# A decoder trunk on one core: the first shift and scale computed from a turned matrix, with 24 units between

## What is computed

```python
for l in range(DEPTH):
    ada = (silu(c) @ w_ada[l] + b_ada[l])           # 2048 -> 6 * 2048
    sh_m, sc_m, g_m, sh_f, sc_f, g_f = split(ada, 6)
    h = x * (1 + sc_m) + sh_m
    y = hybrid_mixer(h, ...)          # h @ w_in[l] (6672 columns), three head groups, @ w_out[l]
    x = layer_norm(ALPHA * x + (1 + g_m) * y, ...)
    h = x * (1 + sc_f) + sh_f
    y = square(relu(h @ w1[l])) @ w2[l]             # 2048 -> 8192 -> 2048
    x = layer_norm(ALPHA * x + (1 + g_f) * y, ...)
```

## Time and profile before

| engine | busy us | share | instructions |
|---|---|---|---|
| TensorE (PE) | 2392.7 | 96% | 13077 |
| TensorE weight load | 2071.0 | 83% | 13077 |
| VectorE (DVE) | 1934.9 | 78% | 2130 |
| ScalarE (ACT) | 1158.8 | 46% | 1504 |
| GpSimd (POOL) | 167.4 | 7% | 120 |

### The profile page before, as it was taken

One profiled execution on the slowest core, in us unless ns is written; L12 is line 12 of the kernel. 1 busy time (PEld: TensorE's weight loads), 2 busy tenths in 40 slices (PEclk: granted clock), 3 DMA queues, 4 the chain that ended last, 5 costly groups with the idle time before them and its releaser, 6 DMA issues.

```text
span 2496.2 us, 32892 instructions
## 1 busy us (share of the span) xinstructions
PE 2392.7 (96%) x13077; PEld 2071.0 (83%) x13077; DVE 1934.9 (78%) x2130; ACT 1158.8 (46%) x1504; POOL 167.4 (7%) x120
## 2 busy tenths in 40 slices
PE   2599999999999999999999999999999999999998
PEld 2599988888888888888879998888888888888886
DVE  7889898877898898889886578778888565655657
ACT  0264475545434435434436446655543443443442
POOL 0002100010011011010010110001001101101001
PEclk9999999999999999999999999999999999999999
DMA  9998577877898898999866546678788666656663
GB/s 388 393 336 300 148 267 261 292 273 270 291 345 308 290 348 306 316 315 313 296 201 177 155 118 202 225 261 282 253 289 301 188 190 193 186 189 192 186 192 119
DMA packets 205054, 633.78 MB, mean 254 GB/s; under 512 B 20237, under 2 KB 20965, under 8 KB 203621
## 3 DMA queue, kind: packets, MB, share of 16 engines
q1 hardware_dynamic: 200320, 614.80, 73.1%
q0 software_dynamic: 3008, 16.32, 1.7%
q10 hardware_dynamic: 1572, 0.56, 0.1%
HBM read 629.50 MB, written 2.10 MB: 253 GB/s over the span
## 4 chain that ended last, share of the span: by engine, by line
PE 90%; DVE 5%; DMA 2%; issue 1%; ACT 1%; SPq 0%; DVEq 0%; ACTq 0%
PE PS L1658 46%; PE PS L1684 17%; PE PS L1686 8%; PE PS L1626 8%; PE PS L1667 4%; DMA RAW<-in_w_ada 2%; PE PS L1640 2%; DVE ACC L1082 1%; DVE WL L1091 1%; PE PS L1715 1%; PE PS L1558 1%; PE PS L1591 1%; DVE CV L1298 0%; DVE ACC L985 0%; DVE MS L1315 0%
## 5 line engine op out<-in xcount | busy, mean ns | idle before, releaser
L686 ACT ACTIVATE WH<-RAW 128x1024 fp32r<-128x1024 f32 (+1 forms) x800 | 831.8, 1044 | 1082.6 <-PE PS L1658 554.6
L1091 DVE TENSOR_TENSOR WL<-RAW,WH 128x1024 fp32r<-128x1024 f32 (+1 forms) x800 | 992.0, 1247 | 431.8 <-ACT WH L686 430.6
L1684 PE MATMUL PS<-HT,WH 128*128 128x512 f32 x1792 | 632.5, 398 | 0.0
L1686 PE MATMUL PS<-HT,WL 128*128 128x256 f32 x1792 | 502.5, 280 | 0.0
L1684 PEld LDWEIGHTS PS<-HT,WH 128*128 128x128 f32 x1792 | 336.5, 188 | 82.3 <-issue 0.5
L985 DVE SCALAR_TENSOR_TENSOR ACC<-ADR,CT,ACC 128x1024 f32<-128x1024 f32 x300 | 392.0, 1307 | 12.3 <-DMA ADR<-in_w_ada 10.4
L1658 PE MATMUL PS<-WH,T2h 128*128 128x512 f32 x1208 | 374.2, 391 | 0.0
L1658 PE MATMUL PS<-WL,T2h 128*128 128x512 f32 x1208 | 372.1, 389 | 0.0
L1658 PE MATMUL PS<-WH,T2l 128*128 128x512 f32 x1208 | 372.0, 389 | 0.0
L1686 PEld LDWEIGHTS PS<-HT,WL 128*128 128x128 f32 x1792 | 338.4, 189 | 0.7 <-issue 0.5
L1658 PE MATMUL PS<-WH,HT 128*128 128x512 f32 x1024 | 288.7, 395 | 0.6 <-issue 0.6
(11 more groups left out here) (297 smaller groups left out, 2035.1 us busy)
## 6 DMA issues: line engine op xcount, KB each, us to landing
RAW<-in_w SPq DMA_DIRECT2D x512, 512.0 KB, 4.1
ADR<-in_w_ada SPq DMA_DIRECT2D x320, 512.0 KB, 5.5
RAW<-in_w_in SPq DMA_DIRECT2D x192, 512.0 KB, 3.9
RAW<-in_w_ada SPq DMA_DIRECT2D x64, 512.0 KB, 15.9
RAW<-in_w_out SPq DMA_DIRECT2D x64, 512.0 KB, 4.9
RAW<-in_w_in SPq DMA_DIRECT2D x32, 264.0 KB, 2.7
GB<-in_b_ada POOLq DMA_DIRECT2D x8, 512.0 KB, 7.3
LNG<-in_ln_g POOLq DMA_DIRECT2D x4, 1024.0 KB, 6.9
```

Source lines behind the costliest of these rows:

```text
L686: act.activation(WH[:, wh_slot(layer, n), 0:w], RAW[:, k, 0:w], ACT.Copy).then_inc(hi_done.sem, 1)
L1091: tt(WL[:, k, 0:w], RAW[:, k, 0:w], WH[:, wh_slot(layer, n), 0:w].bitcast(F32), ALU.subtract).then_inc(lo_done.sem, 1)
L1684: mm(bank(p, j)[:, :], WH[:, wh, cols], HT[:, kt, :, :], start=kt == 0, stop=False, skip_group_check=True)
L1686: ins = mm(bank(p, j)[:, SEQ:2 * SEQ], WL[:, wl, cols], HTh[:, kt, :], start=False, stop=kt == KT - 1, skip_group_check=True)
```

## The change

Quarters 0 to 3 are no longer blocks of 1024 columns. The host lays the first 4096 columns of layer 0's w_ada out as 32 tiles of 128 by 2048 (`ada_first`): a tile has 128 outputs on the partitions and all 2048 inputs along the row. 28 of the tiles go to VectorE: one instruction multiplies the tile by CROW (silu of c, the same on all partitions) and writes the row sums, which are 128 outputs, straight into a column of ADA (`dot`). Four tiles, the first of groups 1 to 4, go to TensorE, as 16 small products each (`first_dot`). x also comes turned from the host (`x_turned`), so that h tiles are made from XT and not from transposes.

The tiles are ordered in eight groups of four, which give shift and scale for two kt each. After a group, its columns are set (`first_cols`), two h tiles are made (`first_tiles`), and units are done: two of pass 0 in groups 0 to 3, two of pass 0 and two of pass 1 in groups 4 to 7. So 24 units are in the queues before the loops begin, which skip them (EARLY). The tiles have four slots (FT) of 1 MB; a slot is loaded again when its tile has been used.

What stood in the first half of pass 1 of layer 0 moves to the second half (PRE), the scaling of X to unit 31, and TensorE waits for LFl ahead of pass 2. Quarter 6 moves from units 0 to 18 to 24 to 35, quarter 7 to 36 to 50, 8 is spread thinly over 51 to 91, 4 moves to 107 to 125, 5 to 126 to 140. X and part of the constants are loaded later, by GpSimd. The counts of the semaphores are adapted; this part is left out here.

```diff
-PRO_SLOTS = 16
+PRO_SLOTS = 4
+FIRST = [[(1, 1), (0, 0), (0, 1), (1, 0)] if 1 <= b <= 4 else [(0, 0), (0, 1), (1, 0), (1, 1)] for b in range(8)]
+FIRST_TILES = [(b, 2 * b + j, which) for b in range(8) for j, which in FIRST[b]]
+BY_TENSOR = [4 * b for b in range(1, 5)]
+BY_VECTOR = [i for i in range(32) if i not in BY_TENSOR]
+FIRST_UNITS = [[(0, 2 * b), (0, 2 * b + 1)] + ([(1, 2 * b - 8), (1, 2 * b - 7)] if b >= 4 else []) for b in range(8)]
+FIRST_ORDER = [u for units in FIRST_UNITS for u in units]
+EARLY = len(FIRST_ORDER)
+PASS0_END = FIRST_ORDER.index((0, 15)) + 1
+PRE = {1: 8, 3: 9, 4: 10, 8: 12, 9: 13, 11: 14, 15: 15}
...
-ADA_PLAN = [[(6, 0, 18), (7, 19, 34), (8, 35, 50), (9, 75, 92), (4, 93, 106), (5, 107, 134),
+ADA_PLAN = [[(6, 24, 35), (7, 36, 50), (8, 51, 92), (9, 93, 106), (4, 107, 125), (5, 126, 140),
...
+SPARSE = [51, 54, 57, 60, 63, 67, 71, 75, 78, 80, 82, 84, 85, 87, 89, 91]
...
+        XT = sb("XT", [P, KT, 2, SEQ], at=place["at"])
...
+        FT = sb("FT", [P, PRO_SLOTS, D], at=t2h_at)
+        CROW = W("CROW", 24, [P, D])
...
+        def tile_used(i):
+
+            if i in BY_TENSOR:
+                return pro_pe.sem, BY_TENSOR.index(i) + 1
+            return pro_dot.sem, BY_VECTOR.index(i) + 1
...
-                if layer == 0 and n < RAW_SLOTS:
-                    sp.wait_ge(ada_mac.sem, 2 + 64 - PRO_SLOTS + n + 1)
-                else:
+                if layer or n >= RAW_SLOTS:
...
-            for a in range(64):
-                if a >= PRO_SLOTS:
-                    sp.wait_ge(ada_mac.sem, a - PRO_SLOTS + 3)
-                dst, arrived = pro_slot(a)
-                sp.dma_start(dst, w_ada_r[(a % 16) * P:(a % 16 + 1) * P, (a // 16) * UW:(a // 16 + 1) * UW]
-                             ).then_inc(arrived, 16)
+            sp.dma_start(CROW[:, :], c.squeeze(0).partition_broadcast(P)).then_inc(pro_crow.sem, 16)
+            n = 0
+            for b in range(8):
+                for i in range(4 * b, 4 * b + 4):
+                    if i >= PRO_SLOTS:
+                        sp.wait_ge(*tile_used(i - PRO_SLOTS))
+                    sp.dma_start(FT[:, i % PRO_SLOTS, :], ada_first[i]).then_inc(pro_tile[i % PRO_SLOTS].sem, 16)
+                    if i % 8 == 0:
+                        t0 = i // 2
+                        sp.dma_start(XT[:, t0:t0 + 4, 1, :], x_turned[t0 * P:(t0 + 4) * P, :].rearrange(
+                            "(t p) n -> p t n", p=P)).then_inc(pro_xt.sem, 16)
+                for p, kt in FIRST_UNITS[b]:
+                    raw_load(0, n, w_in_r[kt * P:(kt + 1) * P, COL0[p]:COL0[p] + UW])
+                    n += 1
...
+            pool.wait_ge(pro_dot.sem, 14)
+            for dst, src in ((LMs[:, :], consts[:, K_LM:K_LM + 1024]), (MLR[:, :], consts[:, K_ML:K_LM]),
+                             (K[:, K_DG:], consts[:, K_DG:K_KEEP])):
+                pool.dma_start(dst, src).then_inc(pro_k.sem, 16)
+            pool.wait_ge(pro_dot.sem, len(BY_VECTOR))
...
+            act.wait_ge(pro_crow.sem, 16)
+            act.activation(CROW[:, :], CROW[:, :], ACT.Silu).then_inc(pro_silu.sem, 1)
...
+            def first_tiles(b):
+
+                act.wait_ge(pro_cols.sem, b + 1)
+                act.wait_ge(pro_xt.sem, 16 * (b // 2 + 1))
+                for kt in (2 * b, 2 * b + 1):
+                    cols, bias, scale = XT[:, kt, 1, :], SH[:, 0, kt:kt + 1], SC[:, 0, kt:kt + 1]
+                    act.activation(HTh[:, kt, :], cols, ACT.Identity, bias=bias, scale=scale).then_inc(hT_hi.sem, 1)
+                    if kt >= 4:
+                        act.wait_ge(hT_ready.sem, hT_ready.at(0, kt - 3))
+                    act.activation(TX[:, kt % 4, :], cols, ACT.Identity, bias=bias, scale=scale
+                                   ).then_inc(hT_tx.sem, 1)
...
+            act.wait_ge(pro_pt.sem, 1)
             act.activation(ACT_IDLE[:, :], PT[:, 0:1], ACT.Identity)
-            for n in range(2):
-                hi_split(0, n)
-            h_tiles(0, 0, 0)
-            for n in range(2, W_SLOTS):
+            n = 0
+            for b in range(8):
+                first_tiles(b)
+                for _ in FIRST_UNITS[b]:
+                    hi_split(0, n)
+                    n += 1
+                if b == 1:
+                    act.wait_ge(pro_dve.sem, 1)
+                    act.activation(LX[:, :], LX[:, :], ACT.Exp).then_inc(pro_act.sem, 1)
+                    act.wait_ge(pro_dve.sem, 2)
+                    act.activation(SIN[:, :, :], ANG[:, :, :], ACT.Sin).then_inc(pro_act.sem, 1)
+                    act.activation(S2[:, :, :], ANG[:, :, :], ACT.Sin, scale=0.5).then_inc(pro_act.sem, 1)
+            for n in range(EARLY, EARLY + AHEAD):
...
+            def dot(i):
+
+                _, kt, which = FIRST_TILES[i]
+                w = FT[:, i % PRO_SLOTS, :]
+                dve.wait_ge(pro_tile[i % PRO_SLOTS].sem, 16 * (i // PRO_SLOTS + 1))
+                stt(w, w, 1.0, CROW[:, :], ALU.mult, ALU.mult, accum_out=ADA[:, ds(16 * which + kt, 1)]
+                    ).then_inc(pro_dot.sem, 1)
+
+            def first_cols(b):
+
+                dve.wait_ge(pro_dot.sem, sum(i < 4 * b + 4 for i in BY_VECTOR))
+                k = 2 * b
+                tt(SH[:, 0, k:k + 2], ADA[:, ds(k, 2)], PT[:, ds(k, 2)], ALU.add)
+                if 4 * b in BY_TENSOR:
+                    stt(SC[:, 0, k:k + 1], ADA[:, ds(16 + k, 1)], 1.0, PT[:, ds(16 + k, 1)], ALU.add, ALU.add)
+                    dve.wait_ge(pro_pe.sem, BY_TENSOR.index(4 * b) + 1)
+                    ins = stt(SC[:, 0, k + 1:k + 2], PB[3 + b][:, 0:1], 1.0, PT[:, ds(17 + k, 1)], ALU.add, ALU.add)
+                else:
+                    ins = stt(SC[:, 0, k:k + 2], ADA[:, ds(16 + k, 2)], 1.0, PT[:, ds(16 + k, 2)], ALU.add, ALU.add)
+                ins.then_inc(pro_cols.sem, 1)
+
+            dve.wait_ge(pro_silu.sem, 1)
+            n = 0
+            for b in range(8):
+                for i in range(4 * b, 4 * b + 4):
+                    if i in BY_VECTOR:
+                        dot(i)
+                    if i == 0:
+                        dve.wait_ge(pro_act.sem, 1)
+                        link(ts(E16[:, :], E16[:, :], 1.0, None, ALU.add))
+                        link(dve.reciprocal(E16[:, :], E16[:, :]))
+                        tt(CT[:, :], E16[:, :], PB[0][:, 0:KT], ALU.mult).then_inc(pro_ct.sem, 1)
+                if b == 0:
+                    dve.wait_ge(pro_pt.sem, 1)
+                first_cols(b)
+                for _ in FIRST_UNITS[b]:
+                    lo_split(0, n)
+                    n += 1
+                h_lo(0, 0, b)
+                if b == 1:
+                    tables()
+                if b == 2:
+                    tables_end()
+                    layer_cols(0)
+                if b == 7:
+                    dve.wait_ge(pro_k.sem, 16 * 3)
+                    dve.tensor_copy(LM[:, :], LMs[:, :]).then_inc(pro_lm.sem, 1)
+            for n in range(EARLY, EARLY + AHEAD):
...
+            def first_dot(b):
+
+                i = 4 * b
+                pe.wait_ge(pro_tile[i % PRO_SLOTS].sem, 16 * (i // PRO_SLOTS + 1))
+                for k in range(KT):
+                    ins = mm(PB[3 + b][:, 0:1], FT[:, i % PRO_SLOTS, k * P:(k + 1) * P], CT[:, k:k + 1], start=k == 0,
+                             stop=k == KT - 1)
+                ins.then_inc(pro_pe.sem, 1)
...
+            pe.wait_ge(pro_ct.sem, 1)
+            n = 0
+            for b in range(8):
+                if 4 * (b + 1) in BY_TENSOR:
+                    first_dot(b + 1)
+                for p, kt in FIRST_UNITS[b]:
+                    if p == 0:
+                        first_unit(0, 0, n, 0, kt, kt == 0, kt == KT - 1)
+                    else:
+                        unit(0, n, n, 1, kt, (HTh, HTl), "rows", kt == 0, False)
+                    n += 1
...
+                    if p == 2 and layer == 0:
+                        pe.wait_ge(hg_lo.sem, hg_lo.at(layer, 1))
...
-                        if p == 0 and kt in H_AT and (layer or H_AT[kt] >= 4):
+                            pe.wait_ge(ada_cols.sem, summed(ADA_DUE[layer][n - 3]))
+                        if p == 0 and kt in H_AT:
                             x_transpose(layer, 0, H_AT[kt])
-                        if at == (1, 8):
+                        if at == pre(layer, 8):
...
+    rows = np.ascontiguousarray(inputs["w_ada"][0, :, 0:2 * D])
+    tiles = []
+    for _, kt, which in FIRST_TILES:
+        w = rows[:, which * D + kt * P:which * D + (kt + 1) * P]
+        tiles.append(w.reshape(KT, P, P).transpose(1, 0, 2).reshape(P, D) if len(tiles) in BY_TENSOR else w.T)
+    laid = {"ada_first": np.ascontiguousarray(np.stack(tiles)), "x_turned": np.ascontiguousarray(inputs["x"][0].T)}
```

More of the change, by code:

```diff
@@ L258, in at @@
                 return self.first + layer * self.per + count
-        raw_in = [Signal(f"raw_in{i}", 0, 16 * 64 // PRO_SLOTS) for i in range(RAW_SLOTS)]
-        raw2_in = [Signal(f"raw2_in{i}") for i in range(PRO_SLOTS - RAW_SLOTS)]
```

(33 more changed lines are left out.)

118 lines of the change are left out of this document (27 added, 91 removed).

## The result

The changed kernel takes 2503.22 us (median; 2498.67 to 2507.96) where the kernel before takes 2496.78 beside it: 1.0026 times as long, interval [1.0017, 1.0034]; it is slower by 6.4 us. The forecast was 2485, range 2472 to 2500. The start came as forecast and better, the loss behind it was 29 us instead of 6.

The account below looks back on a forecast made before the run. It took the kernel as a prologue TensorE waits out, then a gapless queue of units. 161.0 + 2320.2 + 0.8 + 2 + 3 = 2487.0 us for the profiled run, 2.3 less for the median: 2485, range 2472 to 2500.

Parts of the forecast that it names:

- The start: Prologue and first 24 units: VectorE, not DMA, bounds it; these units done at 161.0 us, 16.8 earlier.
- T24: Moment when TensorE has the first 24 units (16 of pass 0, 8 of pass 1) done: 177.8 us before, forecast 161.0.
- A: Rival, start: VectorE's product with sum takes 4.8 us, making the start 57.6 us later, 2542 in all; 8 in 100.
- C: Rival, start: loads bound it, T24 143 and 2467 us at the least, likelier form halfway at 2476; 14 in 100.
- D: Rival, start: units wait until all products are done, T24 near 195, 2519 us in all; 3 in 100.
- (b): Payback in units 24 to 35, where quarter 6 is squeezed in: 2 us, bounds 0 and 7.
- (a): Payback: the turning of quarter 6's sums comes after the first 24 units instead of ahead: 0.8 us.
- the three limits: Units 24 to 35: transfers 35.9 us, VectorE 36.8, ADR slots 35.7, just above TensorE's 35.1.
- The rest keeps or lowers the density: Other moved quarters (q8 spread thinly, q4 later) keep or lower the density of blocks; no loss added.
- (c): Payback at the end of pass 8, quarter 5 in units 126 to 140: 3 us, bounds 0 and 8.
- q4 later: Quarter 4's move to later units, said to keep or lower the density; no loss added.
- rival B: Gain given back: moved quarters starve TensorE at their upper bounds, 15 us instead of 5, 2495 in all; 17 in 100.

Follow-up runs that it names:

- h6: Changed kernel with quarter 6 hollow but for its first block (other 15 loaded and multiplied over 8 columns only): 2495.21 us, 0.9986 of the kernel before.
- h8: Changed kernel with quarter 8 hollow (its 16 blocks loaded and multiplied over 8 columns only): 2496.40 us, 0.9996 of the kernel before.
- h5: Changed kernel with quarter 5 hollow (its 16 blocks loaded and multiplied over 8 columns only, waits kept): 2490.13 us, 0.9969 of the kernel before.
- plan_a: Changed kernel with quarter 8 in units 51 to 77, 9 in 78 to 92, 4 in 93 to 106, 5 in 107 to 134: 2498.06 us.
- h5_dma: Changed kernel with only quarter 5's loads cut to 8 columns, VectorE multiplying all 1024: 2498.84 us, 1.0004 of the kernel before.
- h5_mul: Changed kernel with only VectorE's multiply-adds of quarter 5 cut to 8 columns, blocks loaded whole: 2494.84 us, 0.9989 of the kernel before.
- q9_last: Changed kernel with quarter 9 put last (units 126 to 141), behind quarters 4 and 5, its sum behind the four last units of pass 8: 2491.90 us.

## Why the prediction was wrong

**What bounds the kernel: right.** Outside the start TensorE's time is its work and its few stands, and the lead went mostly where it stood.

**The start: right, short by 6.8 us.** T24 was put at 161.0 and is 154.2. Products take 2.21 us, not 2.4 (24 x 0.19 = 4.6); group 0 was free at 33.3 (forecast 35.1), because AL was done at 27.3 and not at 29, although ScalarE stood longer for it (10.61 us against 6.40). From the last product's end, 136.5 for a forecast 143.2, to T24 it is 17.7 us, as forecast (17.8). The waits for ScalarE (3.09, forecast 3) and the hidden loads (no wait of VectorE for FT between 30 and 140 us) are right too; that DMA would be under 409 GB/s only from group 5 on isn't what happened: 365, 399, 414, 359.

Rivals A, C and D are refuted; T24 came close to the likelier form of C (near 152), but through the faster product, since VectorE did wait for ScalarE in each group and for no tile. The 6.8 us were luck for the total: without them the miss would have been larger by as much. The rule of the Trainium skill, Vector Engine (DVE) Microarchitecture Reference, Points that are easy to get wrong, is contradicted for this form too: two f32 inputs in SBUF with a sum take 2.29 us for 2048 columns, no more for a column than the form without (1.28 us for 1024).

**(b) Quarter 6: inside its bounds.** 5.1 us by this profile (3.8 to 5.1 by those of the other runs that leave it as it is), forecast 2. h6 shows that it is this quarter. The turning of (a) isn't in it: it starts at 196.7, behind the levels, without a wait. The first of the three limits, the transfers, did reach TensorE, but on a path that the sum didn't have: RAW late, ScalarE late by 12.4 us of waits for it, and the banks of pass 1 emptied too late for the levels. X's load, 2.1 MB more, isn't in the 14.7 MB of the sum; loading it early eased the levels by 1.9 us and cost more at the start. X's scaling (3.7 us of ScalarE) stands ahead of those banks too, but h6 has it as well and loses nothing. The new wait for hg_lo is free, as forecast: LFl is written at 175.79, 12 us ahead of the levels.

**"The rest keeps or lowers the density": wrong, 5.4 us.** This is true for the mean over units 51 to 92, not for units 51 to 75, where no block stood and where VectorE's masks are awaited within a unit (h8). Nor is it true for quarter 4, see below.

**(c) Quarter 5: the step that failed.** Forecast 3 us, bounds 0 and 8; the stretch lost 18.4, of which h5 gives back 11.7. That VectorE would be late for this sum was right. Its price was mis-sized twice. First, the slack: the sum does not stand behind unit 140 but directly behind 139, since 140 to 143 come together at the end, and TensorE stood 8.0 us there; I had VectorE 4 us late against a slack of 3, and no row stood behind the 2 us that I added for the loads. Second, what follows a stand: the sum took 1.8 us more at the lower clock, and TensorE then waited 1.5 us for the gate's columns, with no unit between. I had counted a stand by its own length. Together these are 11.3 us.

**Quarter 4: a term put at nothing.** "q4 later" was to keep or lower the density, but its 16 blocks have units 107 to 125, 19 units, where quarter 5 had 28. Around it I count 6.0 us in the same stretch: 2.2 of wait for T2l in pass 7, with blocks between VectorE's WLs right ahead of it; 0.4 of wait for its sum and 2.0 for the sum, which stood ahead of unit 118 before (that one more sum comes behind T24 was (a), at 0.8 us); and 1.4 for its columns. h5 keeps 6.7 us of loss: 2.2 for T2l, 1.9 for quarter 4's sum, and 2.1 for quarter 5's columns. plan_a, with one quarter over 107 to 134 as before, has none of these waits and 78.9 us. So the 6.0 us come with two quarters in the room of one; no run takes quarter 4 out by itself. Of the 18.4 us the two quarters make 17.3; the other 1.1 stay open.

So rival B happened, which had 17 in 100, and beyond its price: 29 us paid back instead of 15 at the most. The gain at the start was real, and its size alone said nothing about the time.

## What to carry to other kernels

When work is moved out of a start into a queue that runs without gaps, look at where its result is awaited before looking at whether the engines have room: 16 blocks over nearly the same units (126 to 139, 126 to 141) cost 11 us more with a gate's sum in TensorE's order behind unit 139 than with a scale's sum in a wait that was there anyway. Give the last place to the result that is needed last. Count a stand of some us by its length, the slow restart and the next wait that no longer has work ahead of it, and judge density by the units in which something is awaited, not by the mean.

## What the runs showed of the hardware

After a stand of some us TensorE restarts at the lower clock. The four matmuls above took 3.69 us after 8.0 us of stand and 3.75 after 5.9 (h5_dma), against 1.96 after 1.4 (h5_mul) and 1.88 without a stand; the 16 of a sum with one column took 3.57 us in plan_a after 4.94 us, in a stretch (340 to 350 us) with a granted clock of 0.58, and 1.84 us in q9_last with no stand ahead of them. Both rows, of plan_a and of q9_last, from the timeline of TensorE:

```profile
342.72 3.57 PE L1625 MATMUL PS<-K,ACC 128*128 128x1 f32 x16 [4.94 <-DVE SB L1487]
```

```profile
556.49 1.84 PE L1628 MATMUL PS<-K,ACC 128*128 128x1 f32 x16
```

In the ten us after (350 to 360) plan_a's clock is 0.91.

A small load can take long while large ones are under way. MD (16 KB), which ScalarE issued at 11.64 us among the tiles of 1 MB, landed 15.5 us later, and ScalarE stood 10.61 us for it; CS (8 KB), issued at 0.75 us ahead of them, took 2.8. That the tiles make the difference is argued: no run leaves them out, and the two loads have different shapes. The Trainium skill, DMA: Bandwidth & Descriptors, Issuing engines are not separate DMA queues, says that issuing from several engines saves only the time of issuing. The trace agrees as far as it goes: MD was issued on ScalarE's queue, the tiles on SyncE's, and it was late all the same.

VectorE's product with sum runs at the pace of the plain one (2.21 us for 2048 columns), and reading the sum (0.08) costs nothing visible.
